# Norm weights of the mixer transposed ahead of the input, the rest inside the first product

## The reference

```
h = x
for i in (0, 1):
    a = rmsnorm(h, norm_mix_pre[i])
    m = nsa_mixer(a, ...) if i == 0 else dilated_mixer(a, ...)
    h = h + rmsnorm(m, norm_mix_post[i])
    f = swiglu(rmsnorm(h, norm_ffn_pre[i]), ffn_w_gu[i], ffn_w_down[i])
    h = h + rmsnorm(f, norm_ffn_post[i])

rmsnorm(x, g) = x * rsqrt(mean(x*x, -1) + 1e-6) * g
```

## Time and profile before

| what | value |
|---|---|
| time, three runs | 884.29, 884.33, 883.52 us, median 884.29 |
| profiled execution | 881.53 us, its span 879.8 us |
| PE busy | 847.1 us, 96% of the span |
| DVE, ACT busy | 536.1 us (61%), 477.6 us (54%) |
| chain that ended last | PE 86%, DVE 8%, DMA 2%, ACT 2%, issue 1% |
| mean granted clock of PE | 0.993 of 2.4 GHz |

### The profile page before, as it was taken

How to read it: one execution, slowest core, us unless ns; L and a number is a source line. 1 busy time by engine, 2 the same in 40 slices (tenths; PEclk the granted TensorE clock), 3 DMA queues, 4 the chain that set the end, 5 groups by cost and what they waited for, 6 DMA issues and landing times.

```text
span 879.8 us, 12217 instructions
## 1 busy us (share of the span) xinstructions
PE 847.1 (96%) x4345; PEld 682.9 (78%) x4345; DVE 536.1 (61%) x1119; ACT 477.6 (54%) x845; POOL 59.9 (7%) x134
## 2 busy tenths in 40 slices
PE   6999999999999999989999999999996999999995
PEld 5898766778888888767887888887874888888874
DVE  5988777686654555577456555555565765555533
ACT  7776666565444453456555555555664554544421
POOL 3000028120000000020000000000001100000002
PEclk9999999999999999999999999999998999999998
DMA  7667100254755645436644354444332457555511
GB/s 257 207 201 238 49 1 1 94 194 136 244 170 191 215 167 191 145 119 215 202 158 131 120 181 141 142 148 144 113 128 95 142 190 241 169 190 186 198 46 48
DMA packets 108542, 135.25 MB, mean 154 GB/s; under 512 B 6304, under 2 KB 92368, under 8 KB 108496
## 3 DMA queue, kind: packets, MB, share of 16 engines
q1 hardware_dynamic: 107824, 132.53, 46.2%
q0 software_dynamic: 576, 2.10, 0.9%
q10 hardware_dynamic: 96, 0.02, 0.0%
HBM read 133.59 MB, written 1.05 MB: 153 GB/s over the span
## 4 chain that ended last, share of the span: by engine, by line
PE 86%; DVE 8%; DMA 2%; ACT 2%; issue 1%; POOL 0%; POOLq 0%; ACTq 0%; SPq 0%; DVEq 0%
PE ps L1495 73%; PE ps L1504 5%; DVE w_lo L1047 4%; PE ps L1688 3%; PE ps L1719 2%; PE ps L1711 1%; DMA w_raw<-in_dil_w_in 1%; DVE xt_lo L1077 1%; DMA w_raw<-in_ffn_w_gu 1%; DVE nt L1060 1%; PE ps L1738 1%; DMA rows<-in_nsa_cmp_pos 1%; DVE tmp L1315 1%; ACT w_hi L600 0%; PE ps L1666 0%
## 5 line engine op out<-in xcount | busy, mean ns | idle before, releaser
L1047 DVE TENSOR_TENSOR w_lo<-w_raw,w_hi 128x1024 fp32r<-128x1024 f32 x248 | 302.9, 1246 | 133.6 <-ACT w_hi L600 131.5
L1495 PE MATMUL ps<-w_hi,xt_hi 128*128 128x512 f32 x760 | 308.5, 406 | 3.4 <-DVE xt_lo L1077 1.9
L1495 PE MATMUL ps<-w_hi,xt_lo 128*128 128x512 f32 x760 | 298.6, 393 | 0.0
L1495 PE MATMUL ps<-w_lo,xt_hi 128*128 128x512 f32 x760 | 298.0, 392 | 0.0
L600 ACT ACTIVATE w_hi<-w_raw 128x1024 fp32r<-128x1024 f32 x248 | 254.3, 1054 | 34.9 <-DMA w_raw<-in_ffn_w_gu 19.2
L1495 PEld LDWEIGHTS ps<-w_hi,xt_hi 128*128 128x128 f32 x760 | 144.3, 190 | 33.0 <-DVE xt_lo L1077 2.7
L1495 PEld LDWEIGHTS ps<-w_hi,xt_lo 128*128 128x128 f32 x760 | 144.0, 189 | 31.3
L1495 PEld LDWEIGHTS ps<-w_lo,xt_hi 128*128 128x128 f32 x760 | 144.5, 190 | 26.7
L853 ACT ACTIVATE st_hi<-ps 128x256 fp32r<-128x256 f32 x44 | 16.8, 383 | 111.6 <-PE ps L1504 111.6
L1495 PE MATMUL ps<-w_hi,st_hi 128*128 128x512 f32 x176 | 69.1, 392 | 2.9 <-DVE st_lo L1340 2.8
L578 POOL TENSOR_TENSOR h<-h,tmp 128x512 f32<-128x512 f32 x16 | 24.1, 1524 | 693.8 <-DVE tmp L1315 693.8
(11 more groups left out here) (188 smaller groups left out, 829.6 us busy)
## 6 DMA issues: line engine op xcount, KB each, us to landing
w_raw<-in_ffn_w_gu SPq DMA_DIRECT2D x88, 512.0 KB, 4.7
w_raw<-in_dil_w_in SPq DMA_DIRECT2D x72, 512.0 KB, 4.5
w_raw<-in_ffn_w_down SPq DMA_DIRECT2D x44, 512.0 KB, 4.1
w_raw<-in_nsa_w_in SPq DMA_DIRECT2D x20, 512.0 KB, 4.5
w_raw<-in_nsa_w_o SPq DMA_DIRECT2D x8, 512.0 KB, 4.9
w_raw<-in_dil_w_o SPq DMA_DIRECT2D x8, 512.0 KB, 3.6
w_raw<-in_nsa_cmp_wk SPq DMA_DIRECT2D x4, 512.0 KB, 4.9
w_raw<-in_nsa_cmp_wv SPq DMA_DIRECT2D x4, 512.0 KB, 4.0
```

What stands on the lines that cost most here:

```text
L1047: dve.tensor_tensor(w_lo[:, n.slot, c:c + 1024], w_raw[:, n.raw, c:c + 1024], w_hi[:, n.slot, c:c + 1024].bitcast(F32), ALU.subtract)\
L1495: ins = pe.matmul(o, s, m, start=start, stop=stop)
```

## The change

`rows` is cut in two tiles with a semaphore each: 16 rows (`norm_mix_pre`) and 32 rows (the rest). PE transposes the 16 before it looks at x; DVE copies 16 columns of `g_t`. PE transposes x block 0, starts `nsa_gemm(0)`, and between its two halves (the `mid` of `gemm`) transposes x block 1 and the 32 rows. DVE copies the other 32 columns after `xt_lo` (1,1). ACT's squares of block 0 move from before the first `xt_out` to behind split 1. PE waits for the second copy before `turn_cmp(0, (2, 4))`, which writes the same PSUM bank.

```diff
-        rows = sb("rows", [48, P], at=at_gp + 3072)
+        rows = [sb("rows_mix", [16, P], at=at_gp + 3072), sb("rows_rest", [32, P], at=at_gp + 3584)]
...
-            act.wait_ge(x_loaded[0], 16)
-            h_squares(0, 0)
             act.wait_ge(gt_ready, 1)
             xt_out(0, 0, 0, 0)
             split(0)
             xt_out(0, 0, 1, 0)
             split(1)
+            act.wait_ge(x_loaded[0], 16)
+            h_squares(0, 0)
             xt_out(0, 1, 0, 0)
             xt_out(0, 1, 1, 0)
...
             dve.wait_ge(rows_t, 1)
-            dve.tensor_copy(g_t[:, :], bank(2, 0, 48)).then_inc(gt_ready, 1)
+            dve.tensor_copy(g_t[:, 0:16], bank(2, 0, 16)).then_inc(gt_ready, 1)
...
             xt_lo_out(0, 1, 1, 0)
+            dve.wait_ge(rows_t, 2)
+            dve.tensor_copy(g_t[:, 16:48], bank(2, 16, 32)).then_inc(gt_ready, 1)
             for m in range(MT):
                 h_rs(0, m)
...
             pe.wait_ge(ident_ready, 1)
-            for m in range(MT):
+            pe.wait_ge(rows_loaded[0], 16)
+            pe.transpose(bank(2, 0, 16), rows[0][:, :], ident[0:16, 0:16]).then_inc(rows_t, 1)
+
+            def turn_x(m):
                 pe.wait_ge(x_loaded[m], 16)
                 for half in range(2):
                     xt_turn(0, m, half, h)
-                if m == 0:
-                    pe.wait_ge(rows_loaded, 48)
-                    pe.transpose(bank(2, 0, 48), rows[:, :], ident[0:48, 0:48]).then_inc(rows_t, 1)
+
+            def turn_rest():
+                turn_x(1)
+                pe.wait_ge(rows_loaded[1], 32)
+                pe.transpose(bank(2, 16, 32), rows[1][:, :], ident[0:32, 0:32]).then_inc(rows_t, 1)
+
+            turn_x(0)
...
-            nsa_gemm(0, N_CMPKV)
+            nsa_gemm(0, N_CMPKV, mid=turn_rest)
             nsa_gemm(1, N_CMPKV)
...
             ins.then_inc(gate_sum, 1)
+            pe.wait_ge(gt_ready, 2)
             turn_cmp(0, (2, 4))
```

More of the change, by code:

```diff
@@ L346, in build @@
         x_loaded = [sem(f"x_loaded{m}") for m in range(MT)]
-        rows_loaded, pos_loaded, w2_loaded = sem("rows_loaded"), sem("pos_loaded"), sem("w2_loaded")
+        rows_loaded = [sem(f"rows_loaded{i}") for i in range(2)]
+        pos_loaded, w2_loaded = sem("pos_loaded"), sem("w2_loaded")
         gw_loaded, out_stored = sem("gw_loaded"), sem("out_stored")
@@ L614, in h_squares @@
                    .then_inc(sq_h[b], 1)
[L617 to L622, removed]
-            act.wait_ge(x_loaded[0], 16)
-            h_squares(0, 0)
+            act.dma_start(rows[0][:, :], norm_mix_pre.rearrange("l (k p) -> (l k) p", p=P))\
+               .then_inc(rows_loaded[0], 16)
+            act.dma_start(rows[1][0:16, :], norm_ffn_pre.rearrange("l (k p) -> (l k) p", p=P))\
+               .then_inc(rows_loaded[1], 16)
+            act.dma_start(rows[1][16:32, :], nsa_cmp_pos[0].rearrange("(k a) d -> k (a d)", a=2))\
+               .then_inc(rows_loaded[1], 16)
             act.wait_ge(gt_ready, 1)
```

## The result

| | before | after |
|---|---|---|
| median of 21 runs each | 883.52 us | 884.95 us |
| profiled execution, its span | 881.53, 879.8 | 884.04, 882.3 |
| gate product starts | 24.88 | 26.86 |

The ratio is 1.0018, interval 1.001 to 1.0026: 0.9 to 2.3 us slower, 1.6 by the middle. The forecast was +0.3 us, told as no change. The time lies in the forecast's range; the size of the change was missed, and the reason is in the first 17 us.

A forecast was written before the change was run, and what follows sets the result against it. The prediction took DVE's opening chain to the end of gw_lo as the bound; +0.1 (last xt_lo) and +0.15 (copy) made about +0.3 us, forecast 884.6 us, no change. Range 882.8 to 886.6.

The forecast's parts named there:

- The bound: Opening on DVE: whatever the change moves the end of gw_lo (24.83 us) by, the span moves by.
- The head: Up to the first product: ACT's first xt_out starts at 5.35 in place of 7.53, a hoped-for 2.2 us.
- ACT and the loads: ACT's queue: piece 1's loads and the squares hold xt_out (1,0) until 14.05; gain 0.1 us and no more.
- PE decides s: s, the start of ACT's eight, follows x block 1's transposes behind twelve matmuls: 14.3, last xt_lo at 17.6, +0.1.
- the lag of 3.85 us: PE's clock rises 3.85 us after the first matmul, as before; the twelve take 4.64 us, ending at 13.6.
- the second case: PE at 1.2 GHz throughout: twelve matmuls end at 14.25, s = 15.35, last xt_lo at 18.65, +1.2 us.
- Small parts: Second g_t copy on DVE ahead of h_rs costs 0.15 us (0 to 0.2); PE's wait for it is free.
- the collision: Piece 2's earlier first load delays piece 1's last half: up to +1.4, taken as none; rival 886.0, chance 0.08.
- late rows: Rival: the 16 rows land behind x, g_t at 6.6, same end, 884.6; chance inside the forecast's 0.50.
- The transposes come late: Rival on PE: clock stays down through the first half, +1.35 us, 885.6; chance 0.17.
- The clock wasn't lost in the pause: Rival: a 2.1 us pause before the gate product drops PE to 1.2 GHz, +2.2, 886.5; chance 0.14.
- The faster case: Rival in the opening: piece 1 lands sooner, clock rises early, DVE's split 1 decides; 883.3 to 882.1, chance 0.11.

The follow-up runs named there:

- e7: e6 plus identity matmuls (4 and 6) that keep PE at work in the opening; ratio to the kernel before 0.9995 (0.9982 to 1.0008).
- e4: Changed kernel plus a one-column activation at the head of ACT's queue, drawing the table load forward; ratio to the kernel before 1.0012 (1.0001 to 1.0024).
- e1: Changed kernel with block 0's squares back at the head of ACT's queue; ratio to the kernel before 1.0009 (0.9997 to 1.0021).
- e3: Changed kernel with squares back at ACT's head and x block 1 transposed ahead of the first product; ratio to the kernel before 0.998 (0.9968 to 0.9991).
- e6: e3 with DVE's two h_rs chains moved from ahead of split 2 to behind gw_lo; ratio to the kernel before 0.9992 (0.9979 to 1.0004).
- e9: e3 once more, unchanged; ratio to the kernel before 0.9979 (0.9967 to 0.9991).
- e11: Kernel before with only x block 1's transposes moved between the halves of the first product; ratio to the kernel before 1.003 (1.0018 to 1.0042).
- e2: Changed kernel with x block 1 and the 32 rows transposed ahead of the first product, squares late; ratio to the kernel before 1.0012 (1.0001 to 1.0022).
- e5: Changed kernel plus identity matmuls (4 and 10) that keep PE at work in the opening; ratio to the kernel before 1.0006 (0.9994 to 1.0017).
- e10: Kernel before with only block 0's squares moved behind split 1; ratio to the kernel before 1.001 (0.9998 to 1.0023).
- e8: Kernel before plus identity matmuls (5 and 4) on PE in the opening; ratio to the kernel before 1.0001 (0.9988 to 1.0013).

## Why the prediction was right or wrong

**The number.** The forecast, 884.6 us, is 0.35 from the measured 884.95, and that closeness is luck. The base was the median of three runs, 884.29; the 21 runs give 883.52. So the base stood 0.8 too high, while the change, 1.4 between the medians, was put at 0.3. "No change" held because even the case that came about was priced below 1.8 us. By its own signs the prediction failed in part: it named as wrong an end of `gw_lo` after 26.5, and it came at 26.82; `xt_out` (1,0) was to start by 15.4 and started at 16.02.

**The bound.** Right for this change: the end of `gw_lo` carries the span. Its shift, +1.98 at 25 us, is +2.13 at 184 and +2.5 at the end. It has a limit the other way: in e7 the gate product starts 3.47 us earlier than before, and the product at 77.42 only 0.34 earlier.

**The head.** Wrong: "ACT's first `xt_out` starts at 5.35 in place of 7.53". It starts at 6.73; the step put the table load at nothing, so 0.8 us of the 2.2 were left. This is the larger miss: with the load back at 2.2 and all else as changed (e4) the gate product stands at +0.91, where about +0.25 was forecast. The Trainium skill (ScalarE: Activation LUTs, "Step-by-step: what each stage is for") says that the load is placed right before the activation that needs it; the traces agree, since the load has the line of the first activation in each. The 1.28 us are in line with its 1283 ns ("What ACT_TABLE_LOAD costs"). The traces show one thing more. Where the first activation stood behind one wait, for a load or the identity (before, e1, e3, e4, e6 to e9, e11), the table load ran at 2.2. Where it stood behind two, for `g_t` and for the x transposes (after, e2, e5, e10), it ran only after the transposes, though in e10 2 us ahead of `g_t`. Whether the number of waits or their kind decides is not shown.

**ACT and the loads.** Right in kind: piece 1 and the squares stand in ACT's way. But with x block 1 inside they decide nothing; in e2 they do. In the changed kernel the splits did not wait for loads, as was forecast, since ACT came to them later and piece 1 landed sooner.

**PE decides s.** Right in kind, and the second, smaller miss. Three cases were given, and the forecast took the lag of 3.85 us seen before. What came about is nearer to the second case, 1.2 GHz throughout (chance 0.17): all but the last of the twelve matmuls ran at the low level, the transposes behind them at the upper one. The forecast had s at about 14.3, and it was 16.02. Of these 1.7 us, 1.36 are the late start of the first product (10.31, not 8.95), which is the head's miss, and 0.43 the clock (5.07 us to the transposes, not 4.64). So the last `xt_lo` end at +1.88 instead of +0.1. The lag wasn't a property to carry over. The last spacing at the low level (0.41 to 0.43) ended 4.8 us after the first product matmul in the changed kernel, e1 and e4, and 4.4 in e11. Where transposes had run up to the product, it ended after 3.6 us (before), 4.0 (e6, e10), 3.2 (e2), 1.5 (e3) and 2.7 (e9), the last two being the same kernel.

**Small parts.** The second copy costs 0.10 (19.36 to 19.45), forecast 0.15. PE's added wait costs nothing. Piece 1's loads land at 9.7 and 11.2 (before: 10.6 and 12.0), although piece 2's first load goes out at 10.20 instead of 10.99: the collision did not come, nor did late rows (they landed at 3.4). The sooner landing isn't the change's doing: in e2, which issues piece 2 at 10.19, the last half of piece 1 landed at 12.1.

**Rivals.** "The transposes come late" was the nearest; with the table load the gate product is at +1.98 and not at +1.35. The clock wasn't lost in the pause. The faster case was shut out by PE (16.02) before the squares could, which ended at 13.7. It came true in e3, where both parts were undone. No rival named the table load.

## What to carry to other kernels

Before moving the first instruction of an engine, look what hangs on it: here the table load moved with the first activation, and it was free only where ACT waited anyway. A transpose that feeds another engine should not stand behind matmuls at the low clock: this kernel's opening ran at 1.2 GHz, and twelve 512-column matmuls there took 5 us. The fastest version measured here is the smallest one: rows transposed ahead of x, neither the squares nor x block 1 moved.

## What the runs showed of the hardware

The loss of clock at the pause near 672 us differs from execution to execution. PE is without work for some 4 us there in each. These are stretches of the kernel before, then of e2 (busy of each engine, with the granted clock third from the end):

```profile
680.00:684.00 4.00, 2.98 (x12) 2.15 (x11) 3.86 (x15) 2.89 (x6) 0.00 (x0) 0.93 0.69 240
684.00:688.00 4.00, 4.00 (x19) 3.30 (x19) 3.69 (x13) 1.24 (x3) 2.19 (x2) 1.00 0.43 143
```

```profile
680.00:684.00 4.00, 3.28 (x8) 2.08 (x8) 3.90 (x15) 2.58 (x7) 0.00 (x0) 0.50 0.70 212
684.00:688.00 4.00, 4.00 (x13) 3.09 (x12) 3.65 (x14) 1.74 (x2) 1.94 (x2) 0.60 0.53 183
```

e2 stays at 0.50 until 687, and its 36 matmuls from 682.38 take 10.74 us where the kernel before takes 8.46. This is 2.3 us, more than the change itself, in one execution; it is why spans of single profiles (e2: 882.4 us) can't rank these kernels. In e8 and e10 the same 36 matmuls took 10.51 and 10.48. In these three the clock also fell later: the first four transposes behind the pause still ran at the upper level,

```profile
675.77 0.66 PE L1507 MATMUL ps<-ident,h 128*128 128x128 f32 x4 [3.96 <-POOL h L579]
677.99 1.11 PE L1507 MATMUL ps<-ident,h 128*128 128x128 f32 x4 [1.55 <-POOL h L579]
```

where the ten other profiles have 1.11 or 1.12 for them. A second pause of 1.1 to 1.6 us follows them, and the next four took 1.11 or 1.12 in all thirteen. So the clock was lost each time, but not at the same point: the prediction's reading, that the pause of 3.96 us alone lost it, holds in ten of them and is open in three. Whether a kernel's shift makes the longer loss more frequent was not tried; the mean clocks of the runs hint at it for e2. It was 0.990 or lower in 7 of its 12 runs, and in 6 of the 35 of the kernel before beside them. The runs at 0.992 have means of 883.64 and 883.86 us, which is level, as the gate product is.
